# Four feed-forward stages with six PSUM banks instead of eight, and three staging buffers instead of four

## The chip, the cores and the metric

The kernel runs on one core of one Trainium2 chip. The metric is the device time of one execution in microseconds (us). A core has five engines with a queue of instructions each: TensorE (PE in the profile; its weight loads are PEld), VectorE (DVE), ScalarE (ACT), GpSimd (POOL) and SyncE (SP, which issues the DMAs). TensorE writes its products to PSUM, which has eight banks of 128 partitions by 512 fp32 numbers. Engines wait for each other with semaphores.

## The reference, cut to what matters

Two transformer blocks run one after the other on 256 tokens of width 1024. The first has a gated delta rule beside a local attention, the second has two layers of three sub-blocks: a feed-forward, a mixer, a feed-forward. The change touches the four feed-forwards of the second block:

```python
def second_block(x, c, ...):
    for l in range(DEPTH_2):                      # 2 layers
        mod = silu(c) @ w_mod[l] + b_mod[l]       # 9 parts: shift, scale, gate of each sub-block
        h = rmsnorm(x) * (1.0 + sc1) + sh1
        x = x + HALF_STEP * g1 * _swiglu(h, ffn1_w_gate[l], ffn1_w_up[l], ffn1_w_down[l])
        h = rmsnorm(x) * (1.0 + sc2) + sh2
        x = x + g2 * _hybrid_mixer(h, ...)
        h = rmsnorm(x) * (1.0 + sc3) + sh3
        x = x + HALF_STEP * g3 * _swiglu(h, ffn2_w_gate[l], ffn2_w_up[l], ffn2_w_down[l])
# _swiglu(h, wg, wu, wd) = (silu(h @ wg) * (h @ wu)) @ wd, 1024 -> 2816 -> 1024
```

## The kernel before

Each engine's program is written out by hand in its own function, and the functions run through the same list of stages. A helper keeps the semaphores: an instruction that ends with `done(ins, key)` publishes a key, and `wait_ge(key)` makes an engine wait until that key has been published. A wait for a key that nobody publishes does nothing.

A product needs more precision than one pass gives, so operands are split in a high and a low part (`hi`, `lo`), and three partial products are added in PSUM.

**PSUM banks.** `bank(key, pool)` gives the next bank of a named pool in turn. Each pool keeps its own turn. If the bank was given out before, TensorE first waits until its last holder is free:

```python
        b = banks[i % len(banks)]
        if b in self.held:
            self.wait_ge(("free", self.held[b]))
```

**One feed-forward** (`pe_ffn`, `act_ffn`, `v_ffn`, `pool_ffn`) has two phases. The gate and up phase goes over 22 column blocks `f` of 128, two at a time: 11 pairs. A pair has four quarters `q`: q 0 and 1 are the gate weights (contraction blocks 0 to 3, then 4 to 7), q 2 and 3 the up weights. In every quarter TensorE does both blocks of the pair (`j` 0 and 1), four contraction blocks each: one matmul of 512 columns (the high weight) and one of 256 (the low weight) for each. So a block (`x`, key `("gu", l, sub, x)`) takes two banks, gate and up, and a pair takes four. Both banks of block `f` are asked for just before its first matmul in quarter 0, both banks of block `f + 1` just before its own first matmul in quarter 0, which comes after the four contraction blocks of block `f`.

When a block is done, ScalarE copies the right halves of its two banks to a staging buffer `SG` (L2073). VectorE adds the left halves (L2124), and this add frees both banks. ScalarE applies silu (L2076), VectorE multiplies gate and up (L2129), ScalarE makes the high part `ahi` (L2080), GpSimd the low part `alo` (L2092), and the staging buffer can be used again. The four staging buffers are quarters of the unused half of the tile `H`.

The same engines prepare the weights. For every quarter of the next pair ScalarE rounds a piece to its high part (L2042) when TensorE has done the same quarter of this pair, and VectorE subtracts to get the low part (L2103). Ahead of the adds of a pair VectorE has the pieces of quarters 0, 1 and 2 in its queue. Between the pieces it takes a share of another job, `v_mods` (L555): rows of the modulation matrix of later sub-blocks are multiplied with the conditioning vector, five ticks to a pair, one multiply of 128x1024 to two ticks. This job is there in all of the first three feed-forwards, and in the fourth only for its first eight multiplies.

The down phase goes over the 22 blocks again and adds to four accumulators (two token blocks by two column halves), whose four banks from the pool `down` are all asked for at once, before the first matmul.

**Around it.** Between two stages `v_join` adds the gated result to `x` and the norm is computed, `pe_turn_in` transposes `x` into banks of the pool `turnf` or `turnx`, and `v_modulated` (L1927) and `act_modulated` (L1936) read these banks into `H`, which frees them. In the numbering (layer, sub-block) the feed-forwards are (0, 0), (0, 2), (1, 0) and (1, 2), and the mixers are (0, 1) and (1, 1). The mixer projects from banks 0 and 1 and ends in the banks 2, 3, 0, 1 of the pool `outx`.

Of the kernel before, what the change touches and what calls it, by code (L numbers as in the profile page):

```python
# [107 lines left out]
ALU, ACT, AX = mybir.AluOpType, mybir.ActivationFunctionType, mybir.AxisListType  # L108
# [104 lines left out]
def plain(a):  # L213
    return a.bitcast(f32)


NS = 5
POOLS = {"all": range(8), "crow": (0, 1), "wb": (4, 5, 6, 7), "ccol": (2, 3), "tx": (4, 5, 6, 7), "six": range(6), "mods": (6, 7), "rest": (0, 1), "att": (2, 3, 4, 5), "bo": (7,), "sq": (4, 5, 6, 7), "low": (0, 1), "tok0": (3, 6, 7, 5), "tok1": (0, 1, 3, 2), "skk": (2,), "sdec": (4, 5), "sq2": (6, 7), "ga": range(8),
         "down": (4, 5, 6, 7), "chain": (2, 3, 4, 5), "proj": (0, 1), "rec": (2, 3), "sd": (4, 5, 6), "dbo": (7,), "outx": (2, 3, 0, 1), "ds": (4, 5, 6, 7), "turnf": (0, 1, 2, 3), "turnx": (6, 7, 4, 5)}


class Store:
# [203 lines left out]
class Tensor(Lane):  # L426
# [6 lines left out]
    def bank(self, key, pool="all"):  # L433
        banks = POOLS[pool]
        i = self.turn.get(pool, 0)
        self.turn[pool] = i + 1
# [3 lines that stand above are left out]
        self.held[b] = key  # L440
        self.M.banks[key] = b
        return self.M.psum[:, b, :]
# [1498 lines left out]


def spare(M):
    return [M.H[:, 2 * i:2 * i + 2, 256:512] for i in range(4)]


def piece(M, i, n):

    return [t[:, i % 4, :].rearrange("p (a b) -> p a b", b=n) for t in (M.WHI, M.WLO)]


def pieces(l, sub):

    out, n = [], 0
    for f in range(0, 22, 2):
        for i in range(2):
            for h in range(2):
                out.append((n, ("fw", l, sub, f, i), 4 * h, 4, 256, h == 1))
                n += 1
    for k0 in range(0, 22, 2):  # L1960
        for h in range(2):
            out.append((n, ("out", ("d", l, sub), k0), h, 1, 1024, h == 1))
            n += 1
    return out
# [72 lines left out]
def act_piece(a, l, sub, p):  # L2037
    M = a.M
    n, key, r0, rn, wd_, _ = p
    hi, _ = piece(M, n, wd_)  # L2040
    a.wait_ge(key, ("staged", l, sub, n - 4))
    a.done(a.e.activation(hi, M.slot(key)[:, r0:r0 + rn, :], ACT.Copy), ("whi", l, sub, n))  # L2042


def act_ffn(a, l, sub):
    M = a.M
    SG = spare(M)

    def emit(p):
        act_piece(a, l, sub, p)  # L2050

    def high(blk, half):
        k, t = slice(4 * half, 4 * half + 4), slice(blk * 128, blk * 128 + 128)
        a.wait_ge(("h", l, sub, blk, half))
        a.done(a.e.activation(M.HHI[:, k, t], M.H[:, k, t], ACT.Copy), ("hhi", l, sub, blk, half))

    first = pieces(l, sub)[:4]
    high(0, 0)
    act_modulated(a, l, sub, 0)
    high(0, 1)  # L2060
    emit(first[1])
    high(1, 0)
    act_modulated(a, l, sub, 1)
    high(1, 1)
    for p in first[2:]:
        emit(p)
    for f in split_all(a, l, sub, emit, None):
        pair = range(f, f + 2) if isinstance(f, int) else ()
        for x in pair:
            key = ("gu", l, sub, x)  # L2070
            b = M.banks[key, 0]
            a.wait_ge(key, ("alo", l, sub, x - 4))
            a.done(a.e.activation(SG[x % 4], M.psum[:, b:b + 2, 256:512], ACT.Copy), ("copied", l, sub, x))  # L2073
        for x in pair:
            a.wait_ge(("summed", l, sub, x))
            a.done(a.e.activation(SG[x % 4][:, 0, :], SG[x % 4][:, 0, :], ACT.Silu), ("silu", l, sub, x))  # L2076
        for j, x in enumerate(pair):
            i = x % 4
            a.wait_ge(("act", l, sub, f + j))
            a.done(a.e.activation(M.AHI[:, f + j, :], SG[i][:, 0, :], ACT.Copy), ("ahi", l, sub, f + j))  # L2080


def pool_ffn(g, l, sub):
    M = g.M
    SG = spare(M)
    for half in range(2):
        k = slice(4 * half, 4 * half + 4)
        g.wait_ge(("hhi", l, sub, 0, half))
        g.done(g.e.tensor_tensor(M.HLO[:, k, 0:128], M.H[:, k, 0:128], plain(M.HHI[:, k, 0:128]), ALU.subtract), ("hlo", l, sub, half))
    for f in range(22):  # L2090
        g.wait_ge(("ahi", l, sub, f))
        g.op(g.e.tensor_tensor(M.ALO[:, f, :], SG[f % 4][:, 0, :], plain(M.AHI[:, f, :]), ALU.subtract), ("alo", l, sub, f))  # L2092


def v_ffn(v, l, sub, work):
    M = v.M
    SG = spare(M)

    def emit(p):
        n, key, r0, rn, wd_, ends = p  # L2100
        hi, lo = piece(M, n, wd_)
        v.wait_ge(("whi", l, sub, n), ("staged", l, sub, n - 4))
        v.done(v.e.tensor_tensor(lo, M.slot(key)[:, r0:r0 + rn, :], plain(hi), ALU.subtract), ("split", l, sub, n),  # L2103
             *([M.freed(key)] if ends else []))

    def low(half):
        k, t = slice(4 * half, 4 * half + 4), slice(128, 256)
        v.wait_ge(("hhi", l, sub, 1, half))
        v.done(v.e.tensor_tensor(M.HLO[:, k, t], M.H[:, k, t], plain(M.HHI[:, k, t]), ALU.subtract), ("hlo", l, sub, half))  # L2109

    first = pieces(l, sub)[:4]
    emit(first[0])
    v_modulated(v, l, sub, 1)
    low(0)
    emit(first[1])
    low(1)
    for p in first[2:]:
        emit(p)
    for f in split_all(v, l, sub, emit, work):
        for j in range(2 if isinstance(f, int) else 0):  # L2120
            i, key = (f + j) % 4, ("gu", l, sub, f + j)
            b = M.banks[key, 0]
            v.wait_ge(("copied", l, sub, f + j))
            v.done(v.e.tensor_tensor(SG[i], SG[i], M.psum[:, b:b + 2, 0:256], ALU.add), ("summed", l, sub, f + j),  # L2124
                   ("free", (key, 0)), ("free", (key, 1)))
        for j in range(2 if isinstance(f, int) else 0):
            i = (f + j) % 4
            v.wait_ge(("silu", l, sub, f + j))
            v.done(v.e.tensor_tensor(SG[i][:, 0, :], SG[i][:, 0, :], SG[i][:, 1, :], ALU.mult), ("act", l, sub, f + j))  # L2129


def pe_ffn(pe, l, sub):
    M = pe.M
    pe.turn["ga"] = 0
    for f in range(0, 22, 2):
        for q in range(4):
            n = 2 * f + q
            hi, lo = piece(M, n, 256)
            k0 = 4 * (q % 2)
            pe.wait_ge(("split", l, sub, n), ("hlo", l, sub, q % 2))  # L2140
            for j in range(2):
                c, key = slice(j * 128, j * 128 + 128), ("gu", l, sub, f + j)
                if q == 0:
                    for i in range(2):
                        pe.bank((key, i), "ga")
                b = M.ps((key, q // 2))
                for kt in range(k0, k0 + 4):
                    low = lambda: pe.mm(b[:, 0:256], lo[:, kt - k0, c], M.HHI[:, kt, :], False, False)
                    if kt:
                        low()  # L2150
                    ins = pe.mm(b, hi[:, kt - k0, c], M.HH[:, :, kt, :], kt == 0, kt == 7)
                    if kt == 0:
                        low()
                if q == 3 and j == 0:
                    pe.done(ins, key)
            pe.done(ins, ("staged", l, sub, n), *([key] if q == 3 else []))
    bs = [[pe.bank(("d", l, sub, blk, hf), "down") for hf in range(2)] for blk in range(2)]
    for k0 in range(19):
        part = [k0] if k0 < 18 else [18, 19, 20, 21]
        pe.wait_ge(("alo", l, sub, part[-1]))  # L2160
        for blk, kt, hf in [(0, k_, h_) for k_ in part for h_ in range(2)] + [(1, k_, h_) for h_ in range(2) for k_ in part]:
            n, c, s = 44 + kt, slice(blk * 128, blk * 128 + 128), slice(hf * 512, hf * 512 + 512)
            hi, lo = piece(M, n, 1024)
            pe.wait_ge(("split", l, sub, n))
            ins = pe.mm3(bs[blk][hf], (M.AHI[:, kt, c], M.ALO[:, kt, c]), (hi[:, 0, s], lo[:, 0, s]), kt == 0, kt == 21)
            if kt == 21 or (blk and hf):
                pe.done(ins, *([("staged", l, sub, n)] if blk and hf else []), *([("d", l, sub, blk, hf)] if kt == 21 else []))
# [804 lines left out]
```

## Time and profile before

| what | value |
|---|---|
| median of 3 runs | 1546.76 us (1543.22 to 1547.25) |
| the profiled execution | 1547.25 us, of which 1545.4 us are the span from the first to the last instruction |
| PE busy | 1461.5 us, 95% of the span |
| DVE busy | 1015.2 us, 66% |
| ACT busy | 697.8 us, 45% |
| POOL busy | 299.9 us, 19% |
| mean granted TensorE clock | 0.972 of full speed |

Busy times of engines overlap, so they don't add up to the span. What is busy all the time sets the time; an idle time on another engine costs nothing unless that engine is waited for. The profile takes one execution, whose time is the highest of the three.

### The profile page before, as it was taken

How to read it: one execution, taken by the hardware profiler on the slowest of the kernel's cores; microseconds unless marked ns; L12 is line 12 of the kernel's file. 1: busy time of each engine (PE TensorE's matmuls, PEld its weight loads, DVE VectorE, ACT ScalarE, POOL GpSimd, SP SyncE). 2: the span in 40 equal slices, each digit the busy share in tenths (PEclk: the TensorE clock that was granted, in tenths of full speed). 3: DMA queues.
4: the chain of work that ended last, by engine and by line, in shares of the span. 5: the costliest groups of instructions: out<-in, count | busy, mean ns of one | idle time of the engine just before them, and what ended most of it. 6: DMA issues, size and time to landing. Idle time of an engine off the chain costs nothing.

```text
span 1545.4 us, 18939 instructions
## 1 busy us (share of the span) xinstructions
PE 1461.5 (95%) x7424; PEld 1127.6 (73%) x7424; DVE 1015.2 (66%) x1531; ACT 697.8 (45%) x1115; POOL 299.9 (19%) x269
## 2 busy tenths in 40 slices
PE   6998999989899999999989999899999999899998
PEld 4557457456688888875678888788887865688887
DVE  4476876634578887455668885688883563786654
ACT  4435230424266553541446663465632631466552
POOL 0423092004111110151411120111101331311100
PEclk9998999979999999999989999999999999999999
DMA  9544443331478888332357978479894422477551
GB/s 384 202 136 136 147 156 121 110 149 55 146 237 300 307 342 288 109 104 88 109 173 268 337 278 331 138 272 314 299 375 141 137 73 94 146 237 255 188 193 55
DMA packets 159641, 306.41 MB, mean 198 GB/s; under 512 B 5952, under 2 KB 115776, under 8 KB 148672
## 3 DMA queue, kind: packets, MB, share of 16 engines
q1 hardware_dynamic: 159120, 304.93, 56.8%
q8 instruction: 58, 0.95, 0.2%
q10 hardware_dynamic: 432, 0.27, 0.1%
q14 instruction: 31, 0.25, 0.0%
HBM read 304.11 MB, written 1.08 MB: 197 GB/s over the span
## 4 chain that ended last, share of the span: by engine, by line
PE 80%; DVE 10%; ACT 5%; POOL 2%; issue 1%; DMA 1%; SPq 0%; DVEq 0%; POOLq 0%; ACTq 0%
PE ps L445 79%; PE ps L448 1%; DVE H L1927 1%; DMA ring<-in_w_first_dram 1%; DVE arena L1293 1%; DVE arena L1290 1%; ACT arena L1557 1%; DVE H L1876 0%; DVE misc L1590 0%; DVE arena L2742 0%; DVE arena L1279 0%; POOL arena L2481 0%; DVE H L1861 0%; DVE X L1867 0%; DVE ring L555 0%
## 5 line engine op out<-in xcount | busy, mean ns | idle before, releaser
L445 PE MATMUL ps<-hh,whi 128*128 128x512 f32 x1408 | 488.7, 401 | 6.0 <-DVE hh L2109 6.0
L2103 DVE TENSOR_TENSOR wlo<-ring,whi 128x1024 fp32r<-128x1024 f32 x264 | 322.0, 1231 | 153.4 <-ACT whi L2042 151.6
L2042 ACT ACTIVATE whi<-ring 128x1024 fp32r<-128x1024 f32 x264 | 274.2, 1055 | 231.2 <-PE ps L445 214.4
L445 PE MATMUL ps<-hh,wlo 128*128 128x256 f32 x1408 | 368.0, 282 | 0.0
L445 PEld LDWEIGHTS ps<-hh,whi 128*128 128x128 f32 x1408 | 254.7, 190 | 55.9 <-DVE hh L2109 6.9
L445 PEld LDWEIGHTS ps<-hh,wlo 128*128 128x128 f32 x1408 | 268.4, 191 | 16.9
L445 PE MATMUL ps<-ring,H 128*128 128x512 f32 (+1 forms) x544 | 237.2, 587 | 10.6 <-ACT arena L2244 5.6
L445 PEld LDWEIGHTS ps<-ring,H 128*128 128x128 f32 x544 | 102.9, 196 | 118.8 <-issue 102.7
L555 DVE SCALAR_TENSOR_TENSOR ring<-ring,cb 128x1024 f32<-128x1024 f32 x144 | 177.0, 1230 | 4.2 <-DMA ring<-in_mods_dram 3.9
L2092 POOL TENSOR_TENSOR alo<-H,ahi 128x256 fp32r<-128x256 f32 x88 | 70.6, 802 | 463.4 <-ACT ahi L2080 459.9
L445 PE MATMUL ps<-H,ring 128*128 128x256 f32 (+1 forms) x576 | 156.5, 430 | 1.5 <-DVE H L1927 0.9
L445 PEld LDWEIGHTS ps<-arena 128*128 128x128 f32 (+3 forms) x1320 | 125.3, 172 | 39.9 <-issue 21.1
L445 PE MATMUL ps<-arena 128*128 128x64 f32 (+6 forms) x1320 | 139.5, 268 | 13.5 <-DVE arena L1604 7.4
L445 PE MATMUL ps<-whi,alo 128*128 128x512 f32 x376 | 145.2, 390 | 0.0
L445 PEld LDWEIGHTS ps<-H,ring 128*128 128x128 f32 x576 | 109.2, 191 | 44.9 <-issue 31.4
L445 PE MATMUL ps<-wlo,ahi 128*128 128x512 f32 x360 | 140.1, 389 | 0.0
L445 PE MATMUL ps<-whi,ahi 128*128 128x512 f32 x352 | 137.0, 389 | 0.0
L445 PEld LDWEIGHTS ps<-whi,alo 128*128 128x128 f32 x376 | 70.6, 188 | 14.8
L445 PEld LDWEIGHTS ps<-wlo,ahi 128*128 128x128 f32 x360 | 67.6, 188 | 14.3
L445 PEld LDWEIGHTS ps<-whi,ahi 128*128 128x128 f32 x352 | 66.1, 188 | 13.6
L2073 ACT ACTIVATE H<-ps 128x512 f32<-128x512 f32 x88 | 52.8, 600 | 48.5 <-PE ps L445 48.5
L2124 DVE TENSOR_TENSOR H<-H,ps 128x512 f32<-128x512 f32 x88 | 57.8, 681 | 5.1 <-ACT H L2073 3.8
(343 smaller groups left out, 1544.4 us busy)
## 6 DMA issues: line engine op xcount, KB each, us to landing
ring<-in_mods_dram SPq DMA_DIRECT2D x76, 1024.0 KB, 5.8
ring<-in_w_in_dram SPq DMA_DIRECT2D x48, 1024.0 KB, 5.2
ring<-in_ffn_w_gate_dram SPq DMA_DIRECT2D x44, 1024.0 KB, 5.5
ring<-in_ffn_w_up_dram SPq DMA_DIRECT2D x44, 1024.0 KB, 7.1
ring<-in_ffn_w_down_dram SPq DMA_DIRECT2D x44, 1024.0 KB, 6.4
ring<-in_w_out_dram SPq DMA_DIRECT2D x12, 1024.0 KB, 4.9
ring<-in_w_first_dram SPq DMA_DIRECT2D x8, 1024.0 KB, 12.6
gates<-gate_rows SPq DMA_DIRECT2D x7, 512.0 KB, 5.8
```

What stands on the lines that cost most here:

```text
L445: return self.e.matmul(o, lhsT, rhs, start=start, stop=stop)
L448: return self.e.transpose(o, in_, self.M.C["ident"])
L555: v.done(v.e.scalar_tensor_tensor(tile, tile, 1.0, M.cvec[p.k], ALU.mult, ALU.mult, accum_out=sums[:, j:j + 1]), ("mod sums", p.n), *([M.f ...
L1290: v.op(v.e.tensor_tensor(t, M.AT[:, k, 0:k].unsqueeze(2).broadcast_to([128, k, w_]), M.XS[:, k, k:32].unsqueeze(1).broadcast_to([128, k, w ...
L1293: v.op(v.e.tensor_tensor(x, x, t, ALU.add))
L1557: a.done(a.e.activation(sm[:, t4, :], sm[:, t4, :], ACT.Exp, bias=nm[:, t4:t4 + 1], accum_out=den[:, t4:t4 + 1]), ("soft", u))
L1927: v.done(v.e.tensor_scalar(M.H[:, k, blk * 128:(blk + 1) * 128], M.ps(key)[:, HS[k]], m[:, cc + k:cc + k + 1], m[:, cs + k:cs + k + 1], AL ...
L2042: a.done(a.e.activation(hi, M.slot(key)[:, r0:r0 + rn, :], ACT.Copy), ("whi", l, sub, n))
L2073: a.done(a.e.activation(SG[x % 4], M.psum[:, b:b + 2, 256:512], ACT.Copy), ("copied", l, sub, x))
L2092: g.op(g.e.tensor_tensor(M.ALO[:, f, :], SG[f % 4][:, 0, :], plain(M.AHI[:, f, :]), ALU.subtract), ("alo", l, sub, f))
L2103: v.done(v.e.tensor_tensor(lo, M.slot(key)[:, r0:r0 + rn, :], plain(hi), ALU.subtract), ("split", l, sub, n), *([M.freed(key)] if ends els ...
L2124: v.done(v.e.tensor_tensor(SG[i], SG[i], M.psum[:, b:b + 2, 0:256], ALU.add), ("summed", l, sub, f + j), ("free", (key, 0)), ("free", (key ...
```

## The change

The pool `ga` of the gate and up phase has banks 0 to 5 in place of 0 to 7, and its turn is no longer set to 0 at the start of each feed-forward. The down phase accumulates in banks 2 to 5 in place of 4 to 7. The pool `turnf` is (6, 7, 0, 1) in place of (0, 1, 2, 3). There are three staging buffers `SG` in place of four, so block `x` uses buffer `x % 3`, and its copy waits for the `alo` of block `x - 3` in place of `x - 4`. Nothing is computed differently.

```diff
-POOLS = {..., "ga": range(8),
-         "down": (4, 5, 6, 7), ..., "turnf": (0, 1, 2, 3), "turnx": (6, 7, 4, 5)}
+POOLS = {..., "ga": range(6),
+         "down": (2, 3, 4, 5), ..., "turnf": (6, 7, 0, 1), "turnx": (6, 7, 4, 5)}
...
 def spare(M):
-    return [M.H[:, 2 * i:2 * i + 2, 256:512] for i in range(4)]
+    return [M.H[:, 2 * i:2 * i + 2, 256:512] for i in range(3)]
...
-            a.wait_ge(key, ("alo", l, sub, x - 4))
-            a.done(a.e.activation(SG[x % 4], M.psum[:, b:b + 2, 256:512], ACT.Copy), ("copied", l, sub, x))
+            a.wait_ge(key, ("alo", l, sub, x - 3))
+            a.done(a.e.activation(SG[x % 3], M.psum[:, b:b + 2, 256:512], ACT.Copy), ("copied", l, sub, x))
...
 def pe_ffn(pe, l, sub):
     M = pe.M
-    pe.turn["ga"] = 0
     for f in range(0, 22, 2):
```

The other lines of the diff write `% 3` for `% 4` wherever `SG` is used (ScalarE's silu and high part, VectorE's add and multiply, GpSimd's low part).

## Rows read from the trace of the kernel before

**Rows 1.** The page: busy times, then the chain that ended last.
```profile
PE 1461.5 (95%) x7424; PEld 1127.6 (73%) x7424; DVE 1015.2 (66%) x1531; ACT 697.8 (45%) x1115; POOL 299.9 (19%) x269
...
PE 80%; DVE 10%; ACT 5%; POOL 2%; issue 1%; DMA 1%; SPq 0%; DVEq 0%; POOLq 0%; ACTq 0%
```

**Rows 2.** Stretch window, length, PE, PEld, DVE, ACT, POOL busy, clock, DMA share, GB/s.
```profile
441.00:554.00 113.00, 113.00 (x644) 98.12 (x643) 96.05 (x134) 69.48 (x102) 14.78 (x20) 1.00 0.87 298
```

**Rows 3.** All waits of PE from 430 to 620 us: total, times, longest.
```profile
PE ps L445 <- DVE H L1876: 2.7, 1, 2.7
```

**Rows 4.** Timeline of ACT: start, duration, line, operands, idle before.
```profile
452.34 0.60 ACT L2073 ACTIVATE H<-ps 128x512 f32<-128x512 f32 x1 [0.28 <-PE ps L445]
...
463.61 0.60 ACT L2073 ACTIVATE H<-ps 128x512 f32<-128x512 f32 x1 [0.28 <-PE ps L445]
...
1390.13 0.60 ACT L2073 ACTIVATE H<-ps 128x512 f32<-128x512 f32 x1 [0.28 <-PE ps L445]
```

**Rows 5.** Timeline of PE, quarter 0 of a pair.
```profile
465.99 0.63 PE L445 MATMUL ps<-hh,whi 128*128 128x512 f32 x2
466.46 0.40 PE L445 MATMUL ps<-hh,wlo 128*128 128x256 f32 x2
```

**Rows 6.** Timeline of DVE, the adds and what is ahead of them.
```profile
454.07 1.27 DVE L2124 TENSOR_TENSOR H<-H,ps 128x512 f32<-128x512 f32 x2
...
464.54 1.21 DVE L555 SCALAR_TENSOR_TENSOR ring<-ring,cb 128x1024 f32<-128x1024 f32 x1
...
465.68 1.27 DVE L2124 TENSOR_TENSOR H<-H,ps 128x512 f32<-128x512 f32 x2
...
1392.17 1.28 DVE L2124 TENSOR_TENSOR H<-H,ps 128x512 f32<-128x512 f32 x2
```

**Rows 7.** Timeline, PE released by DVE at the start of a feed-forward.
```profile
428.64 0.69 DVE L2109 TENSOR_TENSOR hh<-H,hh 128x512 fp32r<-128x512 f32 x1 [0.69 <-ACT hh L2055]
...
429.38 0.50 PE L445 MATMUL ps<-hh,whi 128*128 128x512 f32 x1 [1.96 <-DVE hh L2109]
```

**Rows 8.** Timeline of PE, first matmul of the down phase, feed-forwards 1, 2, 4.
```profile
554.96 0.40 PE L445 MATMUL ps<-whi,ahi 128*128 128x512 f32 x1
...
920.61 0.40 PE L445 MATMUL ps<-whi,ahi 128*128 128x512 f32 x1
...
1481.48 0.40 PE L445 MATMUL ps<-whi,ahi 128*128 128x512 f32 x1
```

**Rows 9.** Timeline of DVE, adds of the last pair, feed-forwards 1, 2, 4.
```profile
555.78 1.28 DVE L2124 TENSOR_TENSOR H<-H,ps 128x512 f32<-128x512 f32 x2
...
921.43 1.28 DVE L2124 TENSOR_TENSOR H<-H,ps 128x512 f32<-128x512 f32 x2
...
1481.15 0.68 DVE L2124 TENSOR_TENSOR H<-H,ps 128x512 f32<-128x512 f32 x1
```

**Rows 10.** Timeline of POOL, low parts of blocks 2 and 3.
```profile
456.27 1.56 POOL L2092 TENSOR_TENSOR alo<-H,ahi 128x256 fp32r<-128x256 f32 x2 [8.90 <-ACT ahi L2080]
```

**Rows 11.** Timeline, start of feed-forward (0, 2).
```profile
793.59 1.49 ACT L1936 ACTIVATE H<-ps,mc 128x128 f32<-128x128 f32 x4
...
796.76 1.05 PE L445 MATMUL ps<-hh,whi 128*128 128x512 f32 x2
```

**Rows 12.** Timeline of PE around idle times of 2.4 us.
```profile
230.25 6.50 PE L445 MATMUL ps<-ring,H 128*128 128x512 f32 x8 [2.43 <-ACT arena L1092]
...
243.59 3.60 PE L445 MATMUL ps<-ring,H 128*128 128x512 f32 x8
...
698.54 1.16 PE L445 MATMUL ps<-arena,ctab 128*128 128x128 f32 x8 [2.40 <-DVE arena L2605]
...
1260.06 2.07 PE L445 MATMUL ps<-arena,ctab 128*128 128x128 f32 x8 [2.41 <-DVE arena L2605]
```

**Rows 13.** Windows behind such an idle time and across shorter ones (clock: third from last).
```profile
230.20:233.00 2.80, 2.75 (x4) 1.22 (x5) 0.54 (x1) 0.00 (x0) 2.64 (x4) 0.50 0.97 404
...
719.00:757.00 38.00, 33.82 (x116) 17.17 (x114) 18.34 (x33) 11.93 (x28) 8.80 (x4) 1.00 0.34 113
```

More of the change, by code:

```diff
@@ L217 @@
 NS = 5
-POOLS = {"all": range(8), "crow": (0, 1), "wb": (4, 5, 6, 7), "ccol": (2, 3), "tx": (4, 5, 6, 7), "six": range(6), "mods": (6, 7), "rest": (0, 1), "att": (2, 3, 4, 5), "bo": (7,), "sq": (4, 5, 6, 7), "low": (0, 1), "tok0": (3, 6, 7, 5), "tok1": (0, 1, 3, 2), "skk": (2,), "sdec": (4, 5), "sq2": (6, 7), "ga": range(8),
-         "down": (4, 5, 6, 7), "chain": (2, 3, 4, 5), "proj": (0, 1), "rec": (2, 3), "sd": (4, 5, 6), "dbo": (7,), "outx": (2, 3, 0, 1), "ds": (4, 5, 6, 7), "turnf": (0, 1, 2, 3), "turnx": (6, 7, 4, 5)}
+POOLS = {"all": range(8), "crow": (0, 1), "wb": (4, 5, 6, 7), "ccol": (2, 3), "tx": (4, 5, 6, 7), "six": range(6), "mods": (6, 7), "rest": (0, 1), "att": (2, 3, 4, 5), "bo": (7,), "sq": (4, 5, 6, 7), "low": (0, 1), "tok0": (3, 6, 7, 5), "tok1": (0, 1, 3, 2), "skk": (2,), "sdec": (4, 5), "sq2": (6, 7), "ga": range(6),
+         "down": (2, 3, 4, 5), "chain": (2, 3, 4, 5), "proj": (0, 1), "rec": (2, 3), "sd": (4, 5, 6), "dbo": (7,), "outx": (2, 3, 0, 1), "ds": (4, 5, 6, 7), "turnf": (6, 7, 0, 1), "turnx": (6, 7, 4, 5)}
 class Store:
@@ L2071, in act_ffn @@
             b = M.banks[key, 0]
-            a.wait_ge(key, ("alo", l, sub, x - 4))
-            a.done(a.e.activation(SG[x % 4], M.psum[:, b:b + 2, 256:512], ACT.Copy), ("copied", l, sub, x))
+            a.wait_ge(key, ("alo", l, sub, x - 3))
+            a.done(a.e.activation(SG[x % 3], M.psum[:, b:b + 2, 256:512], ACT.Copy), ("copied", l, sub, x))
         for x in pair:
             a.wait_ge(("summed", l, sub, x))
-            a.done(a.e.activation(SG[x % 4][:, 0, :], SG[x % 4][:, 0, :], ACT.Silu), ("silu", l, sub, x))
+            a.done(a.e.activation(SG[x % 3][:, 0, :], SG[x % 3][:, 0, :], ACT.Silu), ("silu", l, sub, x))
         for j, x in enumerate(pair):
-            i = x % 4
+            i = x % 3
             a.wait_ge(("act", l, sub, f + j))
@@ L2091, in pool_ffn @@
         g.wait_ge(("ahi", l, sub, f))
-        g.op(g.e.tensor_tensor(M.ALO[:, f, :], SG[f % 4][:, 0, :], plain(M.AHI[:, f, :]), ALU.subtract), ("alo", l, sub, f))
+        g.op(g.e.tensor_tensor(M.ALO[:, f, :], SG[f % 3][:, 0, :], plain(M.AHI[:, f, :]), ALU.subtract), ("alo", l, sub, f))
 def v_ffn(v, l, sub, work):
@@ L2120, in v_ffn @@
         for j in range(2 if isinstance(f, int) else 0):
-            i, key = (f + j) % 4, ("gu", l, sub, f + j)
+            i, key = (f + j) % 3, ("gu", l, sub, f + j)
             b = M.banks[key, 0]
@@ L2126, in v_ffn @@
         for j in range(2 if isinstance(f, int) else 0):
-            i = (f + j) % 4
+            i = (f + j) % 3
             v.wait_ge(("silu", l, sub, f + j))
```

## The prediction

> **What bounds the kernel now.** I read the page first. PE is busy for 95% of the span and makes up 80% of the chain that ended last; every other engine is at 66% or less [rows 1]. Then I looked at the stretches that the change touches, by windows. From 441 to 554 us, ten pairs of the first feed-forward, PE is busy 113.00 of 113.00 us at clock 1.00, while DVE has 96.05 us and the DMA engines 0.87 of their time [rows 2]. The list of PE's waits says the same from the other side: from 430 to 620 us, both phases of that feed-forward, PE waited once, for the join behind it [rows 3]. So here PE is the bound without a gap. What makes PE wait is added to the time one for one, and what relieves ACT, DVE, POOL or a DMA gives nothing. The timeline of ACT shows how even the beat is: the copy of a pair's first block starts at 452.34 and 463.61, 11.27 us apart [rows 4], and it does so through all 44 pairs.
>
> **What the change removes.** Four banks are enough for one pair, so eight banks held two whole pairs. With six, the banks go round by thirds. The first block of a pair gets the third that neither block of the pair before holds. The second block gets the banks that the first block of the pair before has just filled. So PE has a wait that it hadn't: before the second block's first matmul in quarter 0, for VectorE's add of the first block of the pair before. No instruction is added or taken away.
>
> **Is the add in time?** First when PE needs it. In quarter 0 the order of high and low turns once, at the first contraction block, so that two low matmuls stand together. They stand at 466.46, and the high matmul ahead of them, the second of the two in the row at 465.99, started 0.235 us behind the first (0.63 less a matmul's own 0.40), at 466.23 [rows 5]. That is the start of the second block, 2.62 us behind the copy at 463.61 [rows 4]. Then when the add ends. It starts at 465.68, right behind a multiply of the modulation job that started at 464.54 [rows 6]; an add takes 0.68 us, as the single one in [rows 9] does. It ends at 466.36, 0.13 us too late. PE takes up again 0.05 us after a DVE instruction's end (428.64 and 0.69 make 429.33, the matmul stands at 429.38), and this first matmul takes 0.50 us in place of 0.40, since its weights aren't loaded ahead [rows 7]. The stall is 0.13 + 0.05 + 0.10 = 0.28 us here. This pair has the longest distance from copy to add, 2.07 us; the usual one is 2.04, which makes it 0.25 us.
>
> Behind that multiply the add cannot come earlier by PE's being late: the piece ahead of the multiply needs ScalarE's piece of quarter 2, which starts when PE is through quarter 2. All of it shifts with PE, and so the stall comes again in every such pair.
>
> How many are there? Five ticks to a pair and a multiply on every other tick put a multiply right ahead of the adds in each even pair, counted from 0. In an odd pair it is missing: the copy is at 452.34, the need at 454.96, the add ends at 454.07 + 0.68 = 454.75, 0.21 us early [rows 4, 6], and in the other odd pairs it is earlier still. Even pairs with a pair behind them are 0, 2, 4, 6 and 8 in each of three feed-forwards, and 0 and 2 in the fourth, where the job ends with its eighth multiply: 17. The last of them has its copy at 1390.13 and its add at 1392.17, 2.04 us behind [rows 4, 6], and the others lie at 2.03 to 2.07. 17 x 0.25 = 4.3 us. From below the bound is the bare lateness with nothing for taking up again, 17 x 0.10 = 1.7 us; from above all 40 pairs that have one behind them stall so, 40 x 0.28 = 11.2 us. I take 4.3, since the rows give both of its parts.
>
> **The seam to the down phase.** PE asks for all four banks at once and before started right behind the last gate and up matmul [rows 8]. The banks 4 to 7 had been free for long, since the last pair was in 0 to 3. Now they are 2 to 5. As 44 banks leave 2 over 6, the feed-forwards start at turn 0, 2, 4 and 0, and the last pair lies in banks 4, 5, 0, 1, then 0 to 3, then 2 to 5, then 4, 5, 0, 1. So PE waits for the add of block 20 in the first and fourth, and for that of block 21 in the second and third. With the same 0.15 us for taking up again:
> the first, 555.78 + 0.68 + 0.15 - 554.96 = 1.65 us; the second, 921.43 + 1.28 + 0.15 - 920.61 = 2.25 us; the third repeats it to 0.01 us; the fourth, without the modulation job, 1481.15 + 0.68 + 0.15 - 1481.48 = 0.50 us [rows 8, 9]. Together 6.6 us. Nothing later takes them back, since the down phase has no wait of PE to be filled [rows 3]. Nor do VectorE's adds come earlier for it. Only without the 0.15 us each would it be 6.0.
>
> **What I cost at nothing.** The third staging buffer: the copy of a pair's second block waits for the low part of the first block of the pair before. Copies and low parts keep the beat of 11.27 us, so for the pair whose first copy stands at 463.61 it is the first of the two in the row at 456.27 [rows 4, 10], over some 6 us ahead. If that cover were gone, the copy and so the next bank would be late. The shifted start of `ga`: in (0, 2) the second block's banks 4 and 5 hold the transposed `x` of the second token block until ScalarE has read it, which is at 793.59 + 1.49 = 795.08, and the second block starts at 797.2 [rows 11], 2.1 us later. In (1, 0) the same wait was there before, in other banks. `turnf` on 6, 7, 0, 1: all of them are read out before the join, and the mixer's first projection in bank 0 needs the same reads for its own operand. Each of these would cost 1 or 2 us if its cover were gone, and I see nothing they could gain, as no wait of PE named a bank at these places.
>
> **The sum.** 4.3 + 6.6 = 10.9 us on the profiled execution's 1547.25 us makes 1558.2. That execution is 0.5 us above the median of the three, so I forecast 1557.7 us, 0.71% more. With the bounds of the pairs' term it would be 1555.1 and 1564.6. 0.3%, 4.6 us, is about what a measurement of this kernel can tell from no change.
>
> **Rivals.**
>
> *Only the seams cost (0.18).* A wait that comes 0.1 us late may be lost in the pairs, if PE's queue has slack the modelled ends don't show, or if the adds move ahead once PE stands. Against it: the need is read from starts, not from ends. The seams' 6.6 us alone give 1546.8 + 6.6 = 1553.4 us.
>
> *The clock falls behind the seams (0.16).* In this trace three single idle times of PE of 2.40 to 2.43 us stand in dense work. After that at 230.25 eight matmuls of 512 columns took 6.50 us where 3.60 is usual, and at 1260.06 eight small ones 2.07 against 1.16 after that at 698.54, where the clock held [rows 12]; the granted clock was 0.50 behind the first [rows 13], that is 1.2 in place of 2.4 GHz. The second and third seam with 2.25 us are near that. One fall costs 6.50 - 3.60 = 2.9 us, two 5.8: 1560.6 to 1563.5 us.
>
> *The clock swings in the pairs (0.02).* A fall after each of the 17 stalls would be 17 x 2.9 = 49 us and 1607 us. Against it, from 719 to 757 us PE stood still for 4.2 us in several pieces and the clock stayed 1.00 [rows 13]. The Trainium skill, TensorE: Matmul & The Clock Gate, section on psum-queue depth-cycling, tells of just this: short idle times between groups of matmuls, from cycling through the banks, make the clock swing again and again. So far the trace doesn't bear it out.
>
> *Not slower (0.14).* The clock falls near the joins come at some executions' moments and not at others: after nearly equal idle times it fell twice and held once [rows 12]. A later start of each stage can spare such falls. It decides from 10.9 - 4.6 = 6.3 us on, and that is three falls of 2.9 us: 10.9 - 8.7 leaves 2.2 us, 1549.0 us, which reads as no change. For more than 0.3% faster it takes six. For it: the mean clock is below 1, and the three runs lie 4 us apart. Against it: as many falls can be added. 0.11 within 0.3%, 0.03 faster.
>
> *As forecast*, 0.50: 1555 to 1560.5 us.
>
> **How the numbers follow.** Faster 0.03; within 0.3% 0.13 (0.11, and 0.02 of the seams-only case with small seams); slower 0.84. The range leaves out the 49 us case and most of the last rival: from 1551.5, a little below the seams without their 0.15 us each (6.0 us, 1552.8), to 1565.0, a little above two clock falls and the upper bound of the pairs' term.
>
> **What the profile after would show.** PE's waits: two new names, both VectorE's add (L2124), about 21 times in all: 17 of 0.2 to 0.3 us every 22.5 us in the gate and up phases, four of 1.5, 2.1, 2.1 and 0.4 us at the seams. From an even pair's copy to the next copy it would be 11.52 us, from an odd pair's 11.27. POOL and ACT would show no longer waits of their own but the shift. The prediction is wrong if the pairs still keep 11.27 us, if ACT's copy waits for POOL, or if the clock is 0.50 behind a seam.

## The result and the profile after

The changed kernel takes 1557.58 us (median of 5 runs, 1552.69 to 1558.88), the kernel before in the same rounds 1544.91 us (1543.22 to 1547.25). The ratio is 1.0072, 95% interval 1.0049 to 1.0094, so it is slower by 11.1 us (7.6 to 14.5). The forecast was 1557.7 us, 10.9 us more than 1546.76. That it lies 0.1 us beside the measured time is luck in part, since the kernel before took 1.9 us less in these rounds than in the three runs that the forecast started from, and the medians are 12.7 us apart. What can be compared is the difference: 10.9 us forecast, 11.1 us measured, give or take 3.5.

PE's waits in the changed kernel: engine and line, releaser, then total, times and longest (us). One name is new, VectorE's add L2124.

```profile
PE ps L445 <- DVE H L1876: 17.8, 6, 3.1
PE ps L445 <- DVE arena L1604: 7.4, 2, 6.8
...
PE ps L445 <- DVE hh L2109: 5.8, 4, 2.0
PE ps L445 <- DVE H L2124: 5.7, 4, 2.0
```

The four are the seams. Timeline of PE, the first matmul of each down phase, against [rows 8]:

```profile
556.85 0.50 PE L445 MATMUL ps<-whi,ahi 128*128 128x512 f32 x1 [1.40 <-DVE H L2124]
...
923.74 0.50 PE L445 MATMUL ps<-whi,ahi 128*128 128x512 f32 x1 [2.00 <-DVE H L2124]
...
1124.77 0.47 PE L445 MATMUL ps<-whi,ahi 128*128 128x512 f32 x1 [2.04 <-DVE H L2124]
...
1491.71 0.50 PE L445 MATMUL ps<-whi,ahi 128*128 128x512 f32 x1 [0.25 <-DVE H L2124]
```

The idle time in brackets counts from the modelled end of the matmul before, which lies 0.16 us behind the start that the next one would have had (0.40 - 0.24), and the first matmul takes 0.10 us longer. So 1.40 stands for some 1.65 us of time, 2.00 for 2.25, 0.25 for 0.50.

The stalls in the pairs don't show in the list of waits at all: of 0.26 us the modelled ends leave 0.1 us of idle time, too little for the list. They show in the beat. The timeline of ACT has the first copies of pairs 2, 3 and 4, against [rows 4]:

```profile
462.87 0.60 ACT L2073 ACTIVATE H<-ps 128x512 f32<-128x512 f32 x1 [0.28 <-PE ps L445]
...
474.40 0.60 ACT L2073 ACTIVATE H<-ps 128x512 f32<-128x512 f32 x1 [0.28 <-PE ps L445]
...
485.67 0.60 ACT L2073 ACTIVATE H<-ps 128x512 f32<-128x512 f32 x1 [0.28 <-PE ps L445]
```

Behind pair 2 it is 11.53 us, behind pair 3 it is 11.27. The place itself, in the timeline of PE between them, against [rows 5], and VectorE's add ahead of it, against [rows 6]:

```profile
465.26 0.89 PE L445 MATMUL ps<-hh,whi 128*128 128x512 f32 x2
465.98 0.40 PE L445 MATMUL ps<-hh,wlo 128*128 128x256 f32 x2
```

```profile
463.76 1.22 DVE L555 SCALAR_TENSOR_TENSOR ring<-ring,cb 128x1024 f32<-128x1024 f32 x1
464.91 0.08 DVE L555 DVE_READ_ACCUMULATOR ring<-ring,cb 128x1 f32 x1
464.91 1.28 DVE L2124 TENSOR_TENSOR H<-H,ps 128x512 f32<-128x512 f32 x2
```

The two high matmuls take 0.89 us in place of 0.63, 0.26 more. The add starts 2.04 us behind the copy. All 17 places that the prediction named have a beat of 11.52 or 11.53 us, and the 23 others 11.27.

Taken over the trace, from the first to the last copy the four gate and up phases grew by 1.32, 1.29, 1.32 and 0.52 us, 4.4 us in all. From the last copy to the second group of transposes of the next join (in the fourth: to the last matmul) it is 1.64, 3.86, 3.88 and 0.51 us more, 9.9 us in all. The second and third hold more than the wait, since the clock fell there to 0.50, the lower of its two levels (1.2 in place of 2.4 GHz). These are windows behind the two seams, with one more inside the first of them that is all at the low clock; the clock is the third number from the last:

```profile
923.70:926.70 3.00, 2.96 (x8) 2.33 (x9) 2.57 (x5) 2.12 (x4) 2.00 (x2) 0.62 0.00 0
925.00:926.00 1.00, 1.00 (x4) 0.78 (x3) 0.74 (x2) 0.99 (x2) 1.00 (x1) 0.50 0.00 0
1124.80:1127.80 3.00, 3.00 (x9) 2.38 (x10) 2.56 (x5) 2.02 (x4) 2.12 (x2) 0.67 0.25 90
```

Each fall cost 1.6 us (3.86 - 2.25 and 3.88 - 2.25), 3.2 us together. 4.4 + 9.9 = 14.3 us is more than the 10.3 us by which the last matmul is later than in the first trace of the kernel before (1551.47 against 1541.14). The other 4.0 us are stretches that the change doesn't touch and that were shorter here, by clock falls near the joins that didn't come: 2.1 us in the head of the second feed-forward, 1.7 us in the second mixer and 1.0 us ahead of the first feed-forward, with 0.9 us lost in the join before the third. Most of this isn't the change's doing. The second trace of the unchanged kernel (e10, below) lacks the same falls in the head of the second feed-forward and ahead of the first, 2.1 and 1.0 us, and is 4.3 us shorter than the first trace in all. Against that second trace the last matmul of the changed kernel is 14.7 us later, of which 14.3 us are the pairs and the seams.

### The profile page after: what moved, and what is told of

The parts are those of the page before. It is cut to its first block, busy times and chain, and to the rows that moved or that the text cites. A ratio compares the mean times of both kernels' runs of the same rounds, so it can differ in the third digit from the quotient of the medians.

```text
span 1555.8 us, 18934 instructions
## 1 busy us (share of the span) xinstructions
PE 1467.1 (94%) x7424; PEld 1127.3 (72%) x7424; DVE 1017.0 (65%) x1531; ACT 697.0 (45%) x1115; POOL 301.0 (19%) x269
## 4 chain that ended last, share of the span: by engine, by line
PE 79%; DVE 11%; ACT 6%; POOL 2%; issue 1%; DMA 0%; SPq 0%; DVEq 0%; ACTq 0%; POOLq 0%
PE ps L445 78%; PE ps L448 1%; DVE H L1927 1%; DVE arena L1293 1%; DVE arena L1290 1%; ACT arena L1557 1%; DVE ring L555 1%; DMA X<-in_x_dram 0%; DVE H L1876 0%; DVE misc L1590 0%; DVE arena L2741 0%; DVE arena L1279 0%; POOL arena L2480 0%; DVE H L1861 0%; DVE wlo L2103 0%
## 5 line engine op out<-in xcount | busy, mean ns | idle before, releaser
L445 PEld LDWEIGHTS ps<-wlo,ahi 128*128 128x128 f32 x360 | 68.3, 190 | 14.3
L2073 ACT ACTIVATE H<-ps 128x512 f32<-128x512 f32 x88 | 52.8, 600 | 48.3 <-PE ps L445 48.3
L2124 DVE TENSOR_TENSOR H<-H,ps 128x512 f32<-128x512 f32 x88 | 58.2, 681 | 8.2 <-ACT H L2073 8.2
```

The source lines that it names most:

```text
L445: return self.e.matmul(o, lhsT, rhs, start=start, stop=stop)
L2073: a.done(a.e.activation(SG[x % 3], M.psum[:, b:b + 2, 256:512], ACT.Copy), ("copied", l, sub, x))
```

## The experiments

The table gives for each run the ratio to the kernel before of the same rounds, in us of 1544 us, and three sums from its trace against the first trace of the kernel before: pairs (first to last copy, four feed-forwards), seams (last copy to the second group of the next transposes, or to the end), and the rest up to the last matmul.

| run | ratio (95%) | us over before | pairs | seams | rest |
|---|---|---|---|---|---|
| changed kernel | 1.0072 (1.0049 to 1.0094) | 11.1 | 4.4 | 9.9 | -4.0 |
| e7_changed_again | one time, 1559.07 us | - | 4.3 | 9.9 | -2.4 |
| e1_pairs_only | 1.0041 (1.0026 to 1.0056) | 6.3 | 4.5 | 0.0 | -4.0 |
| e11_pairs_only_again | 1.0041 (1.0028 to 1.0054) | 6.3 | 4.5 | 0.0 | -1.3 |
| e12_eight_banks_same_wait | 1.0042 (1.0027 to 1.0057) | 6.5 | 4.5 | 0.0 | -2.7 |
| e2_seams_only | 1.0055 (1.0034 to 1.0076) | 8.5 | 0.0 | 6.9 | -5.4 |
| e3_adds_first | 1.0045 (1.0028 to 1.0061) | 6.9 | 2.4 | 4.9 | -3.1 |
| e4_adds_first_free | 1.0027 (1.0014 to 1.0039) | 4.2 | 2.5 | 0.0 | -2.3 |
| e8_spread_free | 1.0019 (1.0008 to 1.0029) | 2.9 | 0.8 | 0.0 | -1.0 |
| e9_spread_late_ask | 1.0044 (1.0030 to 1.0058) | 6.8 | 0.8 | 2.1 | -2.8 |
| e5_every_pair_late | 1.0112 (1.0074 to 1.0150) | 17.3 | 11.4 | 6.7 | -3.1 |
| e6_three_buffers | 1.0003 (0.9989 to 1.0017) | 0.5 | 0.0 | 0.0 | -2.7 |
| e10_before_again | 0.9997 (0.9987 to 1.0008) | -0.5 | 0.0 | 0.0 | -4.3 |

The rest is negative in all of them: the first trace of the kernel before caught an execution with many clock falls (span 1545.4 us, its second trace 1541.1 us). Columns pairs and seams can be compared to 0.1 us from one trace to another, the rest can't be. Of the seams of e2 0.3 us are no wait for an add: PE stands 0.09 us longer between the two groups of transposes in each of its three joins, and why is open.

### The two waits apart: e1, e11 and e2

e1 and e11 are the changed kernel with the down phase in banks that the last pair doesn't hold:

```diff
+    down = {(0, 0): "down0", (0, 2): "down2", (1, 0): "down4", (1, 2): "down0"}[l, sub]
+    # down0 (2, 3, 6, 7), down2 (4, 5, 6, 7), down4 (0, 1, 6, 7)
-    bs = [[pe.bank(("d", l, sub, blk, hf), "down") for hf in range(2)] for blk in range(2)]
+    bs = [[pe.bank(("d", l, sub, blk, hf), down) for hf in range(2)] for blk in range(2)]
```

The transposes of (0, 1), (1, 0) and (1, 1) go to (4, 5, 0, 1), (0, 1, 2, 3) and (2, 3, 4, 5).

> The changed kernel, but the down phase gets four banks that the last pair doesn't hold, so that the seam has no wait; six banks in the gate and up phase stay. Theory A (the two waits for VectorE's add are the whole cost, 4.4 us in the pairs and 6.6 us at the seams): 17 stalls of 0.26 us stay, the beat is 11.52 us behind even pairs and 11.27 us behind odd ones, there is no wait of PE at the four seams, and the clock stays 1.00 there. Time 4.4 us over the kernel before, give or take the clock falls near the joins. Rival B (the seams are free because what they cost is won back at the joins): no faster than the changed kernel, 11 us over. Rival C (only the seams cost): the time of the kernel before.

> The kernel with waits in the pairs alone once more. It had come out 6.3 us (4.0 to 8.6) over the kernel before, where its trace shows 4.5 us of stalls. Theory A (the 1.8 us are scatter of the clock falls): around 4.5 us this time, with the clock falls at other places than in its first trace. Rival H (six banks cost some 2 us besides that no wait shows): 6 us or more again.

e2 is the kernel before with its eight banks, but with the down phase in (4, 5, 0, 1) in the first and fourth feed-forward and (4, 5, 2, 3) in the others, and with the transposes of (0, 1) in (6, 7, 0, 1).

> The kernel before with eight banks in the gate and up phase, but with the down phase in banks of the last pair, so that it waits for the add of block 20 or 21 as in the changed kernel; three sets of banks for the transposed x keep the joins free of new waits. Theory A: the beat of the pairs is 11.27 us throughout, PE waits at the four seams for 1.40, 2.00, 2.04 and 0.25 us in its rows (1.65, 2.25, 2.25 and 0.50 us of time), 6.6 us over the kernel before, and about 1.6 us more for each seam behind which the clock falls. Rival C (only the pairs cost): the time of the kernel before. Rival D (a wait of 2.0 us is too short for the clock to fall, the falls in the changed kernel came from somewhere else): clock 1.00 behind all four seams.

The traces part the two as theory A has them. In e1 the first copies of pairs 2 and 3 stand 11.53 us apart (timeline of ACT; the edit moved L2073 to L2074), and no seam has a wait:

```profile
464.78 0.60 ACT L2074 ACTIVATE H<-ps 128x512 f32<-128x512 f32 x1 [0.28 <-PE ps L445]
...
476.31 0.60 ACT L2074 ACTIVATE H<-ps 128x512 f32<-128x512 f32 x1 [0.28 <-PE ps L445]
```

In e2 the beat is 11.27 us throughout, and the seams are those of the changed kernel, here the second and third:

```profile
921.15 0.50 PE L445 MATMUL ps<-whi,ahi 128*128 128x512 f32 x1 [1.99 <-DVE H L2124]
...
1117.95 0.50 PE L445 MATMUL ps<-whi,ahi 128*128 128x512 f32 x1 [1.99 <-DVE H L2124]
```

Rivals B and C fall: each half costs by itself, and neither is won back. Rival D got half an answer. Behind both seams of e2 the clock held, as these windows show:

```profile
921.10:924.10 3.00, 2.95 (x13) 2.46 (x14) 2.56 (x5) 2.13 (x4) 2.00 (x2) 1.00 0.00 0
1118.00:1121.00 3.00, 3.00 (x13) 2.48 (x14) 2.56 (x5) 2.06 (x4) 2.09 (x2) 1.00 0.19 76
```

Thirteen matmuls in 3 us here, eight and nine in the changed kernel. After idle times of the same length the clock fell behind both such seams in the changed kernel and in e7, and behind neither in e2 and e5. So an idle time of 2.0 us can bring it down and needn't. Behind the six seams with 1.40 to 1.46 us of idle time (one each in the changed kernel, e7, e2 and e5, two in e3) it held.

Both e1 and e11 come out at 6.3 us where their traces have 4.5 us of stalls. 4.5 us lies within both intervals, but the same 1.8 us twice asked for a test.

### Do six banks cost by themselves: e12

```diff
                 if q == 0:
+                    if f and j:
+                        pe.wait_ge(("summed", l, sub, f - 2))
                     for i in range(2):
                         pe.bank((key, i), "ga")
```

This is in the kernel before, with eight banks.

> The kernel before with its eight banks, its four buffers and its down phase, and only one wait more: before the second block of a pair TensorE waits for the add of the first block of the pair before, which the bank itself doesn't need here. So it has the timing of the run with waits in the pairs alone, and none of its banks. That run was 6.3 us over twice, with 4.5 us of stalls in its trace. Theory A (all that the change costs there is the wait; the other 1.8 us follow from the shift in time, by where the clock falls): about 6 us over again, beat 11.52 us behind even pairs. Rival H (six banks cost some 2 us besides that no wait shows): 4.5 us over.

It comes out at 6.5 us with the same beat:

```profile
462.00 0.60 ACT L2073 ACTIVATE H<-ps 128x512 f32<-128x512 f32 x1 [0.28 <-PE ps L445]
...
473.53 0.60 ACT L2073 ACTIVATE H<-ps 128x512 f32<-128x512 f32 x1 [0.28 <-PE ps L445]
...
484.79 0.60 ACT L2073 ACTIVATE H<-ps 128x512 f32<-128x512 f32 x1 [0.28 <-PE ps L445]
```

So the wait with eight banks comes to the same as the wait with six, and six banks add nothing that these intervals could tell. That isn't a refutation of rival H: its 4.5 us lie within the interval of e12, 4.2 to 8.8 us. It is made less likely by e2 as well, which has eight banks too and comes out 1.6 us over its stalls (8.5 against 6.9, with 5.2 to 11.7 as its interval). What the 1.8 us are made of is less sure. The sections of the trace that move are the heads of the feed-forwards, the joins and the mixers, where the clock is at half speed for some us in every trace, at places that shift: in e12 the first mixer is 2.3 us longer than in the first trace of before and the head of the second feed-forward 2.1 us shorter, the latter as in e10. That a later start of the stages makes more falls on the average fits this, and it is argued, not shown.

### The third buffer: e6

> The kernel before with three staging buffers in place of four and nothing else. Theory A: the low part that the copy waits for is done some 6 us ahead, so no engine waits more: beat 11.27 us, the time of the kernel before within 1 us. Rival F (the copy waits for GpSimd and frees the banks late): ScalarE's copy would show a wait for GpSimd's low part, and each pair would be longer.

Beat 11.27 us, time within 0.2% of the kernel before, and from 430 to 620 us PE has one wait, for the start of the feed-forward:

```profile
PE ps L445 <- DVE hh L2109: 2.0, 1, 2.0
```

The copy waits for no POOL instruction. Rival F falls.

### What makes the add late: e3, e5, e4, e8

These change only `beside`, the number of ticks of the modulation job in each quarter of a pair (before: 1, 1, 1, 2), in the changed kernel; e4 and e8 have the free down banks of e1 as well.

```diff
 def beside(f, q):
-    return 2 if q == 3 else 1
+    return (1, 1, 0, 3)[q]    # e3, e4
+    return (1, 1, 2, 1)[q]    # e5
+    return (2, 1, 0, 2)[q]    # e8, e9
```

> The changed kernel with one tick of the modulation job moved from quarter 2 to quarter 3, behind the adds, so that no multiply stands right ahead of an add; the banks are as in the change. Theory A: each first add starts 0.9 us behind its copy, the beat is 11.27 us throughout (4.4 us won back), the seams shrink to 0.5 us where block 20 is waited for, and to 1.7 us where block 21 is (6.6 becomes 4.4 us). Some 4.4 us over the kernel before. Rival E (it is the number of banks and not the multiply ahead of the add that makes the add late): the beat stays 11.52 us behind even pairs and the time stays 11 us over.

> The changed kernel with one tick of the modulation job moved from quarter 3 to quarter 2, so that a multiply stands right ahead of the adds in every pair that has the job, even and odd. Theory A: the beat is 11.52 us behind all of them; 10 stalls in each of three feed-forwards and 3 in the fourth are 33 x 0.26 = 8.6 us in place of 4.4, the seams stay at 6.6 us, and the time is 4.2 us over the changed kernel. Rival E (the number of banks makes the stall, not the multiply's place): the time and beat of the changed kernel.

> Both mends together: six banks in the gate and up phase and three buffers, adds ahead of the multiply, and a down phase in free banks. Theory A: no wait of PE for an add anywhere, beat 11.27 us, the time of the kernel before within 2 us. If something else in the change costs (the third buffer, the banks of the transposed x, a turn that starts elsewhere), it is left here by itself and shows as more than 2 us.

> As the run with both mends, but the five ticks of a pair go 2, 1, 0, 2 over the quarters in place of 1, 1, 0, 3, so that no pair has two multiplies right behind each other. There the odd pairs' adds had come to stand 1.80 to 2.87 us behind their copies, since VectorE had a backlog, and the pairs still cost 2.5 us. Theory A (a stall is the distance from copy to add less 1.78 us, whatever makes the distance): with one multiply at a time all distances are under 1.78 us, the beat is 11.27 us throughout, no seam waits, and the time is that of the kernel before within 0.15%. Rival H (six banks cost something besides that shows in no wait): still some 4 us over.

Rival E falls: with the number of banks left alone, the stalls follow the multiplies. But my numbers missed. In e3 the even pairs are mended, their adds stand 0.89 to 1.19 us behind the copies where another pair follows, and odd pairs became late in their place, by 1.80 to 2.87 us. The worst is pair 1 of the first feed-forward, here VectorE's timeline:

```profile
449.83 1.22 DVE L555 SCALAR_TENSOR_TENSOR ring<-ring,cb 128x1024 f32<-128x1024 f32 x1
...
450.98 2.35 DVE L2103 TENSOR_TENSOR wlo<-ring,whi 128x1024 fp32r<-128x1024 f32 x2
453.25 1.22 DVE L555 SCALAR_TENSOR_TENSOR ring<-ring,cb 128x1024 f32<-128x1024 f32 x1
454.39 0.08 DVE L555 DVE_READ_ACCUMULATOR ring<-ring,cb 128x1 f32 x1
454.39 1.22 DVE L2103 TENSOR_TENSOR wlo<-ring,whi 128x1024 fp32r<-128x1024 f32 x1
455.53 1.28 DVE L2124 TENSOR_TENSOR H<-H,ps 128x512 f32<-128x512 f32 x2
```

VectorE stands nowhere still: the multiply put behind the adds makes the next pieces late, and the backlog reaches the next pair's add, 2.87 us behind its copy at 452.66. PE's row for it:

```profile
456.27 0.50 PE L445 MATMUL ps<-hh,whi 128*128 128x512 f32 x1 [0.83 <-DVE H L2124]
```

The beat behind this pair is 12.36 us, 1.09 more than 11.27, and 2.87 - 1.78 is 1.09, where 1.78 is the usual distance of 2.04 less its stall of 0.26. Over the pairs of e3, e4, e5 and e8 that rule holds to 0.08 us: at 1.81 us the beat is 11.22 to 11.30, at 2.01 it is 11.43 to 11.49, at 2.04 11.47 to 11.53, at 2.33 11.81. In e5 the adds of the odd pairs stood more than 2.04 us behind their copies, up to 2.61, so they cost 11.4 us where I had 8.6. In e8 five pairs in each of the first three feed-forwards stayed at 1.8 to 2.1 us. The pairs went from 4.4 to 2.4 (e3) and 0.8 us (e8), and not to nothing as expected. So e4 comes to 4.2 us over the kernel before where I had 2 at most, and 2.5 us of them are stalls in the pairs. This window of the changed kernel shows VectorE (the third busy time) with 94.97 us of work in 113 us ([rows 2] has 96.05 for the kernel before), so there is little idle time in which a lateness could vanish:

```profile
441.00:554.00 113.00, 113.00 (x637) 96.99 (x636) 94.97 (x134) 68.37 (x100) 14.82 (x20) 1.00 0.85 295
```

In e3 the seams went to 4.9 us (1.10, 1.67, 1.65, 0.51) where I had 4.4. The second and third are what I expected; in the first, block 20's add stood 1.48 us behind its copy in place of 0.9.

### Banks 6 and 7 left alone, at the least cost: e9

The down banks of the second token block are asked for just before their first matmul, and the second feed-forward takes (4, 5, 2, 3).

```diff
+    bs = [[pe.bank(("d", l, sub, 0, hf), down) for hf in range(2)]]
...
+            if blk and len(bs) == 1:
+                bs.append([pe.bank(("d", l, sub, 1, h_), down) for h_ in range(2)])
```

> The changed kernel with banks 6 and 7 left alone as the change has it, the ticks 2, 1, 0, 2, and the two banks of the second token block in the down phase asked for just before their first matmul, 1.38 us into the phase; in the second feed-forward the first token block takes banks 4 and 5, which are free. Theory A: no stall in the pairs; seams of 0, 0.3, 0.5 and 0 us; 0.8 us over the kernel before. Rival H: as above, 4 us or more over.

Pairs 0.8 us, seams 2.1 us (0.0, 0.7, 1.4, 0.0). Block 20's add wasn't 0.9 but 1.81 us behind its copy in the third feed-forward, so that seam cost 1.4 in place of 0.5. The traces give 3.0 us of stalls, the ratio 6.8 us, with an interval from 4.6 us on. In e8 it is 0.8 us against an interval from 1.2 us on. In these two the interval leaves out what the trace shows. It isn't a fall behind the seams, as both seams with a wait grew by the wait alone (0.36 and 1.16 us in PE's rows). Rival H isn't excluded, and speaks loudest here; against it stand e2 and e12, which are 1.6 and 2.0 us over their stalls with eight banks, and e3 and e5, which are 0.4 and 0.8 us under theirs with six. What the 2 and 4 us are stays open.

### Two traces more: e10 and e7

> The kernel before, run against itself. It gives a second trace of it and tells how far a ratio strays by itself. Theory A: the ratio is 1 within 0.15%; beat and seams are those of the first trace to 0.05 us; what differs is only where the clock is at half speed around joins.

> The changed kernel as it is, for one more trace. Theory A: the beat and PE's waits at the seams are the same to 0.05 us, while the places where the clock falls near joins and seams differ from one execution to the next, so that the span differs by some us. Rival G (the clock falls are fixed by the program): the same falls at the same places.

Against itself the kernel before comes to 0.9997, with an interval of 0.1% (1.6 us) to either side. The spans of its two traces differ by 4.3 us with the same beat and the same seams. In e7 the waits at the seams are 1.40, 1.99, 2.04 and 0.25 us, and the clock fell behind the same two seams as in the first trace of the changed kernel. The two differ by 1.7 us ahead of the first feed-forward and hardly elsewhere. So rival G isn't refuted for the changed kernel: within one kernel most falls came again at their places, and between kernels with the same idle times they didn't.

## Why the prediction was right

**PE is the bound, and a wait is added one for one.** Right. Pairs and seams grew by the stalls, and no stretch of the feed-forwards took anything back.

**17 stalls in the pairs, 4.3 us.** Right in number, place and size: 17 of 0.26 us, 4.4 us. e12 shows that the wait alone makes them.

**Behind a multiply the add doesn't move.** Right, the distance stayed at 2.03 to 2.04 us in all 17. Only the pair of [rows 6] came in from 2.07 us, so its stall is 0.26 us and not the 0.28 of the prediction.

**The seams, 1.65, 2.25, 2.25 and 0.50 us.** Right: 1.64 and 0.51 us in the first and fourth, and 2.24 and 2.26 us in the second and third of e2, which has them without a clock fall (last copy to the first transposes). That is 6.65 us against 6.6.

**Nothing for the buffer and the other banks.** Right for the buffer (e6). For the banks no wait shows in any trace, and e12 against e1 fits it, but with intervals of some 2 us to either side a cost below that isn't excluded.

**The clock.** I had given a fall behind the seams 0.16, at 2.9 us each. It came behind two of them in both traces of the changed kernel. That is the rival, and not the case "as forecast", and I had named a clock of 0.50 behind a seam as a sign that the prediction is wrong. So this term was wrong: my sum had nothing for what came to 3.2 us in the traces. The rival's price was wrong too, 1.6 us each in place of the 2.9 us that I took from the fall at 230.25 [rows 12], where the clock was 0.50 for longer, from 229.12 to 235.95 us, than behind the second seam, from 924.5 to 927.8. The stalls and falls in the trace make 14.3 us, near the upper end of what was measured (7.6 to 14.5). Two of the other executions took only 1552.69 and 1553.59 us; that falls behind the seams didn't come there fits, and isn't shown, since these have no trace. So the forecast met the time closer than its terms deserve. The case "not slower" isn't borne out: 4.0 us were spared elsewhere, but the unchanged kernel's second trace is 4.3 us shorter than its first in the same way. The rival of a clock that swings in the pairs falls: from 441 to 554 us of the changed kernel, with five stalls in it, the granted clock was 1.00. The Trainium skill, TensorE: Matmul & The Clock Gate, section on psum-queue depth-cycling, tells of a kernel whose clock swings because short stops between groups of matmuls come often enough. It doesn't say how often or how long; five stops of 0.26 us in 113 us didn't do it here.

**What the profile would show.** Wrong in one point: I had expected the 17 stalls in the list of PE's waits. The modelled ends of the matmuls cover 0.16 of their 0.26 us. And I had expected the clock at 1.00 behind the seams.

## What to carry to other kernels

In this kernel a bank is free when its last reader has ended, and a reader that is in time with two whole sets was 0.1 us late with one and a half; so before a pool is cut, compare the start that the second user will have with the end of the read, in the beat of the slowest pair, and add the cost of taking up again. Look at the seams by themselves: the four waits there that ask for all banks of the next phase cost 6.6 us, more than the 17 in the loop with 4.4. And with VectorE at 85% of its time, moving its side job off one deadline put it on the next.

## What the runs showed of the hardware that I had not expected

- After an idle time of PE of 1.99 to 2.04 us in dense work the clock fell to 0.50 in four cases (changed kernel, e7) and held at 1.00 in four (e2, e5); each fall cost 1.6 us. After 1.40 to 1.46 us it held in all six.
- A stall of 0.26 us leaves no row of its own in the trace: the matmul ahead of it is modelled 0.16 us beyond the start of its successor, and only the distance between starts shows it.
- Two traces of one unchanged kernel differ by 4.3 us in span, all of it outside the four feed-forwards' pairs and down phases, which keep to 0.01 us.
